# Three pieces of the weight stream of a two-layer trunk with experts, multiplied in float32 from where they landed

## The reference, cut to what matters

```python
def swiglu(x, wg, wu, wd):
    return (jax.nn.silu(x @ wg) * (x @ wu)) @ wd

def moe_swiglu(x, w_router, we_gate, we_up, we_down):
    logits = (x @ w_router).astype(jnp.float32)
    top_vals, top_idx = lax.top_k(logits, TOP_K)
    gates = jax.nn.softmax(top_vals, axis=-1)
    combine = jnp.einsum("bske,bsk->bse", jax.nn.one_hot(top_idx, N_EXPERTS, dtype=jnp.float32), gates)
    out = jnp.zeros_like(x)
    for e in range(N_EXPERTS):
        out = out + combine[..., e:e + 1] * swiglu(x, we_gate[e], we_up[e], we_down[e])
    return out
...
x = layer_norm(ALPHA * x + ffn, ln2_g[i], ln2_b[i])
```

## Time and profile before

| | |
|---|---|
| median of three runs | 1282.82 us |
| profiled execution: time, span | 1281.19 us, 1279.5 us |
| busy: TensorE, VectorE, ScalarE | 96%, 87%, 73% of the span |
| HBM read | 428.40 MB, 339 GB/s over the span |
| granted TensorE clock, mean | 0.997 |

### The profile page before, as it was taken

How to read it: one execution, slowest core, us unless ns; L and a number is a source line. 1 busy time by engine, 2 the same in 40 slices (tenths; PEclk the granted TensorE clock), 3 DMA queues, 4 the chain that set the end, 5 groups by cost and what they waited for, 6 DMA issues and landing times.

```text
span 1279.5 us, 15891 instructions
## 1 busy us (share of the span) xinstructions
PE 1222.3 (96%) x6199; PEld 1051.8 (82%) x6199; DVE 1112.1 (87%) x871; ACT 937.3 (73%) x720; POOL 50.0 (4%) x57
## 2 busy tenths in 40 slices
PE   9999999999999999999999999999999999999785
PEld 8988888888989888888787877878888788887563
DVE  6978555568889999999999999999999999999897
ACT  5575444454867787888878888888888778878774
POOL 0100000001010000000000000000000000000130
PEclk9999999999999999999999999999999999999998
DMA  9947655537459999999999999999999999999992
GB/s 320 343 161 263 195 183 184 195 122 244 169 173 342 376 409 394 403 412 410 410 405 406 411 410 413 407 394 409 412 410 410 410 404 411 409 412 402 411 412 116
DMA packets 143556, 434.49 MB, mean 340 GB/s; under 512 B 8964, under 2 KB 50996, under 8 KB 131188
## 3 DMA queue, kind: packets, MB, share of 16 engines
q1 hardware_dynamic: 139936, 421.07, 85.7%
q0 software_dynamic: 3456, 12.32, 2.8%
q10 hardware_dynamic: 84, 0.02, 0.0%
HBM read 428.40 MB, written 4.98 MB: 339 GB/s over the span
## 4 chain that ended last, share of the span: by engine, by line
PE 59%; DMA 17%; DVE 16%; ACT 5%; issue 3%; SPq 0%; DVEq 0%; ACTq 0%
DVE w_lo L1027 13%; DMA raw<-in_we_down 9%; PE turn L1691 7%; PE turn L1693 6%; PE turn L1692 6%; DMA raw<-in_we_gate 6%; PE accp L1691 5%; PE accp L1692 5%; PE accp L1693 5%; PE turn L1803 4%; PE turn L1800 4%; ACT w_hi L657 4%; PE turn L1802 2%; PE turn L1801 2%; PE turn L2117 2%
## 5 line engine op out<-in xcount | busy, mean ns | idle before, releaser
L1027 DVE TENSOR_TENSOR w_lo<-raw,w_hi 128x1792 fp32r<-128x1792 f32 (+3 forms) x449 | 900.8, 2040 | 93.1 <-ACT w_hi L657 87.7
L657 ACT CAST w_hi<-raw 128x1792 fp32r<-128x1792 f32 (+2 forms) x443 | 760.0, 1725 | 171.0 <-DMA raw<-in_we_down 42.5
L2117 PE MATMUL turn<-w_hi,t_both 128*128 128x448 f32 x512 | 192.9, 377 | 25.3 <-DVE w_lo L1027 18.0
L2118 PE MATMUL turn<-w_lo,t_both 128*128 128x448 f32 x512 | 186.9, 365 | 0.0
L1691 PE MATMUL turn<-w_hi,a_hi 128*128 128x448 f32 x496 | 183.9, 371 | 0.0
L1693 PE MATMUL turn<-w_hi,a_lo 128*128 128x448 f32 x496 | 181.7, 366 | 0.0
L1692 PE MATMUL turn<-w_lo,a_hi 128*128 128x448 f32 x496 | 181.6, 366 | 0.0
L2117 PEld LDWEIGHTS turn<-w_hi,t_both 128*128 128x128 f32 x512 | 96.1, 188 | 49.1 <-issue 19.6
L2118 PEld LDWEIGHTS turn<-w_lo,t_both 128*128 128x128 f32 x512 | 96.3, 188 | 7.2
L1691 PEld LDWEIGHTS turn<-w_hi,a_hi 128*128 128x128 f32 x496 | 93.1, 188 | 9.6
L1692 PEld LDWEIGHTS turn<-w_lo,a_hi 128*128 128x128 f32 x496 | 93.2, 188 | 8.4
(11 more groups left out here) (291 smaller groups left out, 1539.5 us busy)
## 6 DMA issues: line engine op xcount, KB each, us to landing
raw<-in_we_gate SPq DMA_DIRECT2D x128, 896.0 KB, 8.6
raw<-in_we_up SPq DMA_DIRECT2D x128, 896.0 KB, 9.3
raw<-in_we_down SPq DMA_DIRECT2D x96, 1024.0 KB, 9.5
raw<-in_w_in SPq DMA_DIRECT2D x18, 1024.0 KB, 7.0
raw<-in_we_down SPq DMA_DIRECT2D x32, 512.0 KB, 6.2
raw<-in_w_down SPq DMA_DIRECT2D x11, 1024.0 KB, 5.0
raw<-in_w_gate SPq DMA_DIRECT2D x10, 1024.0 KB, 5.2
raw<-in_w_up SPq DMA_DIRECT2D x10, 1024.0 KB, 5.3
```

Source lines behind the costliest of these rows:

```text
L657: nc.scalar.copy(w_hi[:, p % PARTS, 0:filled(p)], raw[:, p % RING, 0:filled(p)]).then_inc(hi_done, 1)
L1027: return nc.vector.tensor_tensor(out, whole, hi.bitcast(f32), ALU.subtract)
L2117: nc.tensor.matmul(to[:, c, :], few, wh[:, kk, c, :], start=(k == 0), stop=False)
L2118: last = nc.tensor.matmul(to[:, c, :], few, wl[:, kk, c, :], start=False, stop=(k == KD - 1))
```

## The change

Three pieces are never split: down piece 427 (unit 29, pair 2), gate piece 430 (unit 31, pair 1) and up piece 436 (unit 31, pair 3). TensorE multiplies them in plain float32 out of `raw`. One float32 matmul stands where two `fp32r` ones stood. ScalarE and VectorE leave these pieces out of their lists, and SyncE loads the piece six places later when TensorE has used the unsplit one, not when VectorE has split it. Which piece follows which is as before on every engine.

```diff
+    WHOLE = {PLACE[piece] for piece in (("down", N_UNITS - 3, 2), ("gate", N_UNITS - 1, 1), ("up", N_UNITS - 1, 3))}
...
         def split_of(p):
 
-            return (first_split, (4, 6)[p]) if p < 2 else (split_done, p - 1)
+            assert p not in WHOLE
+            return (first_split, (4, 6)[p]) if p < 2 else (split_done, p - 1 - whole_before(p))
+
+        def freed(p):
+
+            return (piece_used, upto(p)) if p in WHOLE else split_of(p)
...
                 if p >= RING:
-                    sp.wait_ge(*split_of(p - RING))
+                    sp.wait_ge(*freed(p - RING))
...
             def split_hi(p):
 
+                if p in WHOLE:
+                    return
...
             def split_lo(p):
-                dve.wait_ge(hi_done, p - 1)
+                if p in WHOLE:
+                    return
+                dve.wait_ge(hi_done, p - 1 - whole_before(p))
...
+            def unsplit(p):
+
+                pe.wait_ge(slot_filled[p % RING], 16 * fills(p))
+                return raw[:, p % RING, 0:filled(p)]
...
+            def few_down_whole(i, pair):
+
+                _, s = expert_step(i)
+                w = unsplit(down_piece(i, pair)).rearrange("p (j d) -> p j d", d=D)
+                for j, block in enumerate(blocks_of(pair)):
+                    for c in range(2):
+                        last = nc.tensor.matmul(accp[:, 2 + c, :], hT_packed[:, block, :].bitcast(f32),
+                                                w[:, j, c * BANK:(c + 1) * BANK], start=(s == 0 and block == 0),
+                                                stop=(s == QUARTERS - 1 and block == BLOCKS - 1))
+                last.then_inc(piece_used, 1)
+
+            def few_rows_whole(i, which, pair):
+
+                e, _ = expert_step(i)
+                to = (gate_banks, up_banks)[which]
+                w = unsplit((up_piece if which else gate_piece)(i, pair)).rearrange("p (k c f) -> p k c f", k=2, c=2)
+                for kk in range(2):
+                    k = 2 * pair + kk
+                    for c in range(2):
+                        last = nc.tensor.matmul(to[:, c, :], xg_few[e % 2][:, k, :].bitcast(f32), w[:, kk, c, :],
+                                                start=(k == 0), stop=(k == KD - 1))
+                last.then_inc(piece_used, 1)
```

More of the change, by code:

```diff
@@ L140, in down_piece, with whole_before @@
         return PLACE["down", i, pair]
+    WHOLE = {PLACE[piece] for piece in (("down", N_UNITS - 3, 2), ("gate", N_UNITS - 1, 1), ("up", N_UNITS - 1, 3))}
+    def whole_before(p):
+        return sum(q < p for q in WHOLE)
     def blocks_of(half):
@@ L2107, in rows_pair @@
             def rows_pair(i, which, pair):
+                if (up_piece if which else gate_piece)(i, pair) in WHOLE:
+                    few_rows_whole(i, which, pair)
+                    return
                 kind, (e, _) = ORDER[i], expert_step(i)
@@ L2128, in down @@
                     pe.wait_ge(e_hT_lo, i + 1)
+                if down_piece(i, pair) in WHOLE:
+                    few_down_whole(i, pair)
+                    return
                 add = few_down_pair if light(i) else down_pair
```

## The result

The changed kernel has a median of 1287.88 us over six runs (1286.10 to 1289.16), the kernel before 1282.49 (six runs, 1281.83 to 1283.02). The ratio is 1.0036, interval 1.0026 to 1.0045. So it is slower by 0.36%, 4.6 us by the ratio, where no change that could be told was forecast (+0.9 us at 1283.4 against this median), and 1287.88 lies above the range, which ended at 1286.0. The profiled execution took 1286.10 us, its span is 1284.4 us against 1279.5, and it was the fastest of the six; the others took up to 3.1 us longer.

The account below looks back on a forecast made before the run. Weight bytes bound the expert block, so only the last units could change: the gather chain gained 2.1 us, but the later cast chain decided at +0.6. Forecast 1281.8 us profiled, 1283.4 median; range 1281.6 to 1286.0.

Parts of the forecast that it names:

- What bounds the kernel: Weight bytes bind the expert block; only the stretch from the last pieces' landing to the end can change.
- the chain shown: Profile's last-ending chain: gather of more_rows, add_rows(3) at 1245.70, splits of 438 and 439, times_up at 1251.39.
- The cost of a float32 product: Four passes on TensorE: about 3.0 us per 448-column piece, plus 1.4 for 430 and 436, plus 1.6 for 427.
- Rival 1: Float32 product costs no more than the split one: times_up moves by -0.8 us, time 1282.0; chance 0.08.
- Pieces 427 and 430: Unit 30's times_up begins near 1224.0, gather 3 at 1226.5, 2.6 us earlier; 430 ends about where it was.
- If the gather takes its 16.45 us again it lands at 1243.0: Last gather of rows, started 2.6 us earlier at 1226.5, was assumed to keep its duration.
- rival 2: A later load of 433 leaves a DMA hole: 0.5 to 1.5 us more, time 1283.9 to 1284.9; chance 0.2.
- Piece 436: 435 begins again at 1242.07; 436 takes 3.0 us for 1.63, so VectorE can take 439 at 1249.7.
- Chain of the cast: 1249.7, +0.6: 439's cast, behind 436's product and the low-rows copy, decides: times_up and the end come 0.6 us later.
- the lead: Before the change, the gather chain was 0.8 us later at 439 than the chain through 436's product.
- Rival 3: TensorE idles 3.9 us ahead of 435 and its clock falls: +1.7 to +4.7 us, time 1285.1 to 1288.1; chance 0.2.
- The loads: Loads wait for TensorE: 442 issued at 1247.1, a hole of about 1 us, landing at 1252.1, covered by 2.3.

Follow-up runs that it names:

- the version with twelve fills: Changed kernel plus twelve fp32r matmuls on TensorE ahead of piece 435, results never read: median 1286.65 us, ratio 1.0024 to the kernel before.
- the three versions of before: Kernel before with eight unread matmuls ahead of 435, 1281.91 us; with SiLU ahead of 437's cast, 1282.81; with SiLU first, more unread matmuls and add_rows(3) moved, 1280.66.

## Why the prediction was wrong

**What bounds the kernel.** Right. DMA share stays at 1.0 until 1246, and only the last units changed. The chain from 437's landing through SiLU and 436 to the cast of 439, found beneath the chain shown, was the one that decided.

**The cost of a float32 product.** Right: at full clock records of 448 columns stand 0.376 us apart, two to a matmul, so eight of them take 3.0 us, for 2.99 to 3.12; those of 512 columns stand 0.429 us apart, and 427 took 3.43 for 3.41. That is four passes, as "FP8 and Floating Point Precision" of the Trainium skill, TensorE Precision Notes, has it; the half rate of "Perfetto Trace Analysis", Engine Utilization, in the same skill holds for each of the two records and not for the matmul. Rival 1 is out.

**Pieces 427 and 430.** The order of events held: `times_up` of unit 30 at 1223.50 (forecast 1224.0), gather 3 from 1226.04 (1226.5). What I didn't price is the gather's own bytes. "437 lands when its bytes have come, 1239.31 again: the stream is full" was the first step that failed: a full stream is just where 0.5 MB put ahead of 437 costs it 1.29 us. Behind it stands "If the gather takes its 16.45 us again it lands at 1243.0": it took 8.9 us and landed at 1234.9, because GpSimd issued it in 2.6 us. I had looked at the loads for a hole, and there was none up to 437; rival 2 had the size (0.5 to 1.5 us) by way of a hole and named the gather only in passing.

**Piece 436.** "TensorE again begins 435 at 1242.07. 436 then takes 3.0 us" was the step that made the miss. It takes the granted clock as given, so the clock stands in the sum at nothing. TensorE began at 1243.16 and at 1.2 GHz. The sum's "Chain of the cast: 1249.7, +0.6" is right for what it counts, 1.38 for the float32 product less the 0.73 of the lead; the two terms that it lacks measured 1.3 (the late 437) and 2.9 (the clock), and 0.65 + 1.29 + 2.93 are the 4.87.

**Rival 3** was the case. Its mechanism, place and sign are right: VectorE's backlog gone, so a longer pause, so a lower clock at 435. Its pause was 3.9 us and came out as 4.92, since 437 was late by 1.1 on top; its price of 1.7 to 4.7 holds the 2.9 that the clock took. It had a chance of 0.2, and the reasons against it were one undisturbed execution and a pause of 2.5 us in it. The version with 436 alone unsplit shows a fall behind such a pause, and all twelve runs of the change lie above the range. The range was therefore too narrow from above: I had half of that rival left out.

**The loads.** 442 was issued at 1251.14 instead of the 1247.1 forecast, since TensorE was through with 436 only at 1251.0, and the DMA engines stood nearly idle from 1247 to 1252. It still cost nothing: the cast of 442 (1258.41) followed the first half of the last h (1258.14) with no wait, as forecast.

## What to carry to other kernels

Where one engine is relieved, look at what its backlog was filling on the others. TensorE's pause grew by 2.4 us here, 1.1 of them the late 437, and the largest loss, 2.9 us, was in the work behind the pause. A pause that in one profile leaves the clock alone is not proof that it does so in each run: 2.54 us did here, 2.59 us did not. Where such a pause stands ahead of work on the chain, the clock belongs in the forecast, at a price of up to the work behind the pause once over (2.9 us here, of the 4.7 that 435 and 436 take at full clock). And if a transfer is let go earlier into a full stream, count its bytes against whatever lands behind it, and don't take its time from issue to landing as fixed.

## What the runs showed of the hardware

- The clock fell at different places in different executions of nearly the same program: in the profile of the version with twelve fills from 1198.1 to 1204.9 and at 1256, of the changed kernel from 1198.1 to 1204.9 and at 1242.5. Six of the fourteen profiles have a fall around 1200. It shows no cost by 431: its cast began at 1224.07 in the changed kernel, with such a fall, and at 1224.27 in the kernel before, without.
- A gather of 0.5 MB kept GpSimd for 8.8 us in all profiles with 427 split (kernel before, only 436, and the three versions of before) and for 0.9 to 2.6 us in all with 427 unsplit, where VectorE had gaps. Gaps alone don't explain it: the gather ahead of it was issued in 2.5 us in the kernel before, beside a VectorE that worked without a gap. The cause was not tried. It matters here, since with the short issue the bytes moved ahead of piece 437.
